# A two-block kernel: the first 64 modulation panels, summed on VectorE and TensorE, moved wholly to TensorE in 32-row column tiles

## What is computed

```
c_act = silu(c)                                    # (1, 2048)
mod = c_act @ w_ada + b_ada                        # w_ada: 2048 x 12288
sh1, sc1, g1, sh2, sc2, g2 = split(mod, 6)         # six vectors of 2048
h = rms_norm(x, norm_mix_g) * (1 + sc1) + sh1
proj = h @ w_in                                    # the first large product
...
x = x + g1 * (merged @ w_out)                      # first block, then the second
```

## Time and profile before

| | |
|---|---|
| median of three runs | 3482.86 us |
| the profiled execution | 3486.62 us |
| its span (first to last instruction) | 3484.8 us |
| VectorE busy | 2892.9 us, 83% |
| TensorE busy | 2341.4 us, 67% |
| GpSimd busy | 1267.6 us, 36% |
| ScalarE busy | 1008.8 us, 29% |

### The profile page before, as it was taken

The page is one execution under the profiler, slowest core; times in us unless marked ns, Lnnn a source line. Parts: engine busy times, 40 slices in busy tenths (PEclk is TensorE's granted clock), DMA queues, the critical chain, the costliest instruction groups (busy, mean ns, idle before and its releaser), DMA issues.

```text
span 3484.8 us, 37714 instructions
## 1 busy us (share of the span) xinstructions
PE 2341.4 (67%) x14550; PEld 1985.7 (57%) x14550; DVE 2892.9 (83%) x3487; ACT 1008.8 (29%) x1529; POOL 1267.6 (36%) x975
## 2 busy tenths in 40 slices
PE   8869999988999999998989889000044420003444
PEld 8858999977888888887979779000011110001111
DVE  7698867877897887888668767899999999998777
ACT  1404443434645454554565444000000000000000
POOL 6351101100110110110000001578867788886663
PEclk7779999999999999998999999555577765556766
DMA  9517978967887997984553346899999999999997
GB/s 363 205 32 269 348 255 305 339 254 247 301 327 266 329 320 273 323 311 164 175 169 110 105 149 223 343 398 420 420 420 420 420 420 421 421 420 421 420 420 319
DMA packets 223692, 1069.00 MB, mean 307 GB/s; under 512 B 24345, under 2 KB 30489, under 8 KB 157593
## 3 DMA queue, kind: packets, MB, share of 16 engines
q0 software_dynamic: 119808, 704.70, 51.1%
q1 hardware_dynamic: 103704, 361.89, 28.9%
HBM read 1062.82 MB, written 3.67 MB: 306 GB/s over the span
## 4 chain that ended last, share of the span: by engine, by line
PE 51%; DVE 18%; POOL 14%; DMA 11%; issue 4%; ACT 2%; DVEq 0%; POOLq 0%; SPq 0%; ACTq 0%
PE ps L597 50%; POOL wide L1751 6%; DMA wide<-in_up,idx_t 5%; DVE acts L2648 4%; POOL wide_b L1751 4%; POOL raws L1751 3%; DMA raws<-in_up,idx_t 2%; DMA wide_b<-in_up,idx_t 2%; DMA a_raws<-in_ada 1%; DVE wide L2576 1%; POOL a_acc L1751 1%; DVE a_raws L2505 1%; DVE a_acc L1791 1%; ACT acts L1291 1%; DVE raws_r L1767 1%
## 5 line engine op out<-in xcount | busy, mean ns | idle before, releaser
L597 PE MATMUL ps<-opa_both,w_hi 128*128 128x256 f32 (+1 forms) x5024 | 1152.0, 318 | 58.3 <-DVE opa_both L1867 31.5
L1767 DVE TENSOR_TENSOR raws_r<-raws,w_hi 128x1024 fp32r<-128x1024 f32 x607 | 729.9, 1223 | 233.3 <-ACT w_hi L1230 229.2
L597 PEld LDWEIGHTS ps<-opa_both,w_hi 128*128 128x128 f32 x5024 | 831.8, 194 | 124.5 <-issue 59.0
L597 PE MATMUL ps<-opa_both,raws_r 128*128 128x256 f32 x3152 | 883.7, 285 | 0.0
L1230 ACT ACTIVATE w_hi<-raws 128x1024 fp32r<-128x1024 f32 x607 | 638.0, 1057 | 672.8 <-PE ps L597 429.9
L597 PEld LDWEIGHTS ps<-opa_both,raws_r 128*128 128x128 f32 x3152 | 608.6, 193 | 7.4
L1666 POOL DMA_DIRECT2D a_raws<-in_ada x320 | 169.2, 529 | 1166.3 <-DVE a_acc L1791 920.0
L597 PE MATMUL ps<-opb_both,w_hi 128*128 128x512 f32 (+1 forms) x1952 | 578.2, 362 | 5.1 <-DVE opb_both L2471 4.8
L597 PE MATMUL ps<-opb_both,raws_r 128*128 128x256 f32 x1616 | 442.6, 282 | 0.0
L1791 DVE SCALAR_TENSOR_TENSOR a_acc<-a_raws,csil,a_acc 128x1024 f32<-128x1024 f32 x317 | 401.1, 1297 | 20.9 <-DMA a_raws<-in_ada 20.8
L597 PEld LDWEIGHTS ps<-opb_both,w_hi 128*128 128x128 f32 x1952 | 342.9, 190 | 58.7 <-DVE opb_both L2471 5.7
(11 more groups left out here) (445 smaller groups left out, 3340.2 us busy)
## 6 DMA issues: line engine op xcount, KB each, us to landing
raws<-in_w SPq DMA_DIRECT2D x607, 512.0 KB, 4.6
a_raws<-in_ada POOLq DMA_DIRECT2D x320, 512.0 KB, 5.7
a_raws<-in_ada SPq DMA_DIRECT2D x28, 512.0 KB, 9.1
raws<-in_ada SPq DMA_DIRECT2D x24, 512.0 KB, 10.8
acts<-in_ada SPq DMA_DIRECT2D x12, 512.0 KB, 8.8
x_res<-in_xT SPq DMA_DIRECT2D x1, 2048.0 KB, 13.0
out<-x_res SPq DMA_DIRECT2D x2, 1024.0 KB, 24.0
wide<-in_up,idx_t POOLq DMA_INDIRECT x109, 28.9
```

The lines of the kernel that those rows point to most:

```text
L597: return nc.tensor.matmul(out, lhs, rhs, start=start, stop=stop)
L1767: TT(w_lo[p % RAW].rearrange("p b n -> p (b n)"), raw[p % RAW], w_hi[p % HI][:, :, :].rearrange("p b n -> p (b n)").bitcast(F32), ALU.subt ...
```

## The change

All 64 panels of group 0 are summed by TensorE with the panel as the moving operand. `first_steps` does two matmuls a panel, each with 512 moving columns; the stationary operand is `csil_rows[:, k, :]`, column k of `csil` repeated 32 times (made once by a new VectorE copy, in room that later belongs to `opa_both`). Half a panel goes to column tile j = 2(h mod 2) + half, so that two successive panels of one pair fill the four column tiles of a bank: bank 4 for h = 0 and 1, bank 7 for h = 2 and 3. Over k the matmuls accumulate in PSUM. Then `ada_rows(0, 4)` and `ada_fold(0)` make columns of the rows, as for the other groups. VectorE's 43 steps, `pair_sums` and the first matmul into bank 7 (with zeros from `stat`) are gone. Every place of group 0 is now released by TensorE alone, by one count per panel. The order of loads is the same.

Two tensors are made longer (`quarter` from 4 to 32 columns, `fold_r` from 128 to 256 bytes a partition), by which `raws`, `a_raws`, `a_acc`, `wide`, `acts` and `wide_b`, into which panels and gathered rows land, start at a multiple of 256 bytes; before, all of them started 32 bytes past one.

```
-ON_PE = [q for q in range(64) if q < 4 or q % 7 in (1, 4)]
+FIRST_STEPS = 64
...
 def place_free(q):
     before = [r for r in range(q) if PLACES[r] == PLACES[q]]
-    return STEPS[before[-1]][:2] if before else None
+    return before[-1] + 1 if before else None
...
-fold_r = sb("fold_r", [P, 2, 4, 4])
+fold_r = sb("fold_r", [P, 2, 32])[:, :, 0:16].rearrange("p r (c s) -> p r c s", c=4)
...
+csil_rows = wide[:, 5, 1024:1536].rearrange("p (k m) -> p k m", k=DC)
...
+            def first_steps(q0, q1):
+                for q in range(q0, q1):
+                    h, k = first_group(q)
+                    pe.wait_ge(aland[PLACES[q]], 16 * USE[q])
+                    for half in range(2):
+                        j = 2 * (h % 2) + half
+                        m = mm(ps[32 * j:32 * j + 32, (4, 7)[h // 2], :], csil_rows[:, k, :],
+                               place[PLACES[q]][:, half * 512:(half + 1) * 512], k == 0, k == DC - 1)
+                    m.then_inc(S["adan"], 1)
...
-            mm(ps[:, 7, 0:32], ident, stat[:, 0, :], True, False)
-            pe.wait_ge(S["csl"], 2)
-            direct_steps(0, 8)
+            pe.wait_ge(S["csl"], 3)
+            first_steps(0, 8)
             norm(0)
-            direct_steps(8, 44)
-            pair_sums(0, STEPS[31][1] if 31 not in ON_PE else STEPS[30][1])
-            direct_steps(44, 64)
-            pair_sums(2, BY_DVE).then_inc(S["adaps"], 1)
+            first_steps(8, 64)
+            ada_fold(0)
...
+            V.tensor_copy(csil_rows, csil[:, 0, :].unsqueeze(2).broadcast_to([P, DC, 32])).then_inc(S["csl"], 1)
...
-            ada_steps(0, 16)
-            norm_rows(lambda j: ada_steps(16 + 4 * j, 20 + 4 * j))
-            ada_steps(48, 64)
+            norm_rows()
             rest_to(2)
+            ada_rows(0, 4)
             ada_cols(0)
```

More of the change, by code:

```diff
@@ L285 @@
 CON_N = (("ident", P), ("swap", P), ("rope_cos", T), ("rope_sin", T), ("causal", 3 * P), ("cmp_add", 2 * 16),
-         ("cmp_mul", 2 * 16), ("bucket", 384), ("iota16", 16), ("fold", 32), ("quarter", 4))
+         ("cmp_mul", 2 * 16), ("bucket", 384), ("iota16", 16), ("fold", 32), ("quarter", 32))
 def _consts():
@@ L355, in constants @@
     put("fold", np.tile(np.eye(32, dtype=np.float32), (4, 1)))
-    put("quarter", np.repeat(np.eye(4, dtype=np.float32), 32, 0))
+    put("quarter", np.tile(np.repeat(np.eye(4, dtype=np.float32), 32, 0), (1, 8)))
     put("iota16", np.broadcast_to(np.arange(16, dtype=np.float32), (P, 16)))
@@ L537, in load_a @@
                 if place_free(q):
-                    name, count = place_free(q)
-                    sp.wait_ge(S[name], count)
+                    sp.wait_ge(S["adan"], place_free(q))
                 half, k = first_group(q)
@@ L543, in load_first @@
             def load_first(p):
-                name, count = STEPS[[q for q in range(64) if PLACES[q] == HALVES + p][-1]][:2]
-                sp.wait_ge(S[name], count)
+                sp.wait_ge(S["adan"], [q for q in range(64) if PLACES[q] == HALVES + p][-1] + 1)
                 load_w(p)
@@ L680, in ada_sums @@
             def ada_sums(g, banks):
-                pe.wait_ge(S["ada"], 64 * (g + 1) - len(ON_PE))
+                pe.wait_ge(S["ada"], 64 * (g + 1) - FIRST_STEPS)
                 pe.wait_ge(S["adacol"], g)
@@ L691, in ada_fold @@
             def ada_fold(g):
-                pe.wait_ge(S["adafold"], g)
+                pe.wait_ge(S["adafold"], g + 1)
                 for i in range(4):
@@ L1664, in load_a @@
                 if q >= EARLY + HALVES:
-                    pool.wait_ge(S["ada"], q - HALVES + 1 - len(ON_PE))
+                    pool.wait_ge(S["ada"], q - HALVES + 1 - FIRST_STEPS)
                 pool.dma_start(a_raw[q % HALVES], a["ada"][q]).then_inc(bland[q % HALVES], 16)
@@ L1774, in ada_steps @@
                 for q in range(q0, q1):
-                    if q in ON_PE:
-                        continue
                     g, k, h = q // 64, q % 64 // HALVES, q % HALVES
[L1778 to L1782, removed]
-                    else:
[L1784 to L1791, removed]
+                    dve.wait_ge(bland[h], 16 * ((q - EARLY) // HALVES + 1))
+                    c = csil[:, g // 3, k:k + 1]
+                    if k == 0:
+                        ins = TS(a_acc[:, h, :], a_raw[h], c, None, ALU.mult)
+                    else:
+                        dve.wait_ge(S["ada"], q - HALVES + 1 - FIRST_STEPS)
+                        ins = STT(a_acc[:, h, :], a_raw[h], c, a_acc[:, h, :], ALU.mult, ALU.add)
                     ins.then_inc(S["ada"], 1)
             def ada_rows(g, b0):
-                dve.wait_ge(S["adarow"], g)
+                if g:
+                    dve.wait_ge(S["adarow"], g)
+                else:
+                    dve.wait_ge(S["adan"], FIRST_STEPS)
                 wide_e = a_acc[:, 0, :].rearrange("p (r a i) -> p r a i", r=2, i=32)
@@ L1802, in ada_rows @@
                     ins = TT(fold_e[:, r], fold_r[:, r].unsqueeze(1).broadcast_to([P, 4, 4, 4]),
-                             cst("quarter").unsqueeze(2).unsqueeze(2).broadcast_to([P, 4, 4, 4]), ALU.mult)
+                             cst("quarter")[:, 0:4].unsqueeze(2).unsqueeze(2).broadcast_to([P, 4, 4, 4]), ALU.mult)
                     if r == 0:
@@ L1823, in ada_cols, with norm_rows @@
                    ALU.add).then_inc(S["adacol"], 1)
-            def norm_rows(beside):
+            def norm_rows():
                 dve.wait_ge(S["ss"], 1)
@@ L1831, in norm_rows @@
                 for j in range(8):
-                    beside(j)
                     s = slice(2 * j, 2 * j + 2)
```

## The result

The changed kernel ran in 3448.94 us (median of four, 3446.68 to 3451.09), 35.0 us under the kernel before, whose median is 3483.97 with one more run added. The ratio is 0.9897, 95% interval [0.9879, 0.9916]. The forecast was 3467 us, range 3456 to 3477: the direction was right, and of the 35.0 us gained it had 15.8. The profiled execution's span fell from 3484.8 to 3445.6 us, by 39.2.

What follows compares the result with a forecast made beforehand. The first stage was taken as bound by loads waiting for their places, not by DMA's rate. Loads 10.8 us and tail 5.0 us made 15.8 us, taking the median from 3482.86 to 3467.1 us, range 3456 to 3477.

Steps and rivals of the forecast that it cites:

- the one on alignment: Landing places of panels and gathers: starting them at a multiple of 256 bytes was taken to gain 0.
- fitted 6.9 ns: Fixed part of a piece's DMA time, from panels of 4 KB pieces at 411 GB/s and gathers of 8 KB at 420.
- The bound of 24 us: Gathers: alignment can take no more than a piece's fixed part, 2.2% of their 1100 us.
- The rows of 1 KB pieces: Loads to `sg` (aligned) landed in 5.1 us, to `acts` (32 bytes past) in 5.7; nearest rows on alignment, mostly latency.
- The rival on alignment: Gathers: one unused beat a piece saved, 4.2 us more, 3463 us; by the whole bound 3443; chance 0.12.
- Loads and places: Group 0 loads: places released in time, 411 GB/s from 24 us on, last panel at about 100.6, 10.8 us earlier.
- The tail: From last panel's landing to the end of `gain`: 6.1 us instead of 11.14, 5.0 less (6.2 at the high clock).
- That all the rest shifts whole: From the first block's product on, everything waits for `gain` and shifts by the full 15.8 us.
- The slower rival: Group 0 sums on TensorE: column tiles don't overlap, low clock stays, 1.9 us a panel, 23 us slower, 3506; chance 0.06.

Runs made afterwards that it cites:

- a1: The changed kernel with the two lengthened tensors at their old lengths, landing places again 32 bytes past a multiple of 256, sums still on TensorE: 3469.21 us, ratio 0.9958.
- b2: The kernel before with the first `pair_sums` moved behind the step of panel 57 instead of panel 43: 3483.25 us, ratio 0.9997.

## Why the prediction was wrong

*The step that failed* is the one on alignment: "I take 0, since the rows of both sizes fit one fixed cost, which is what a piece would have anyway". Both rates came from pieces at the same 32 bytes past a multiple, so the fit could not tell what the place costs. What the runs showed in its place: 17.2 us less in the gathers by the trace, 20.3 in all when done alone. Nor does the place's cost come out of the fitted 6.9 ns: with the rates on the multiple, 420 and 427, the same fit still has 2 x 156.0 - 307.0 = 5.1 ns, since a piece of 4 KB lost 3.5 ns (159.5 to 156.0) and one of 8 KB 5.1 (the rates are rounded to 1 GB/s, so these are good to some tenths of a ns). The bound of 24 us held, though not by its reason; giving it a chance of 0.12, and only a third of its size in the range, was the mistake. The rows of 1 KB pieces, by the prediction's own words mostly latency, could not speak for or against it.

*The rival on alignment* had the sign, the stage and the condition (a share of 1.01). Its price of 4.2 us was a quarter of the measured one.

*Loads and places.* Right in mechanism: gaps gone, the rate the bound. In size, a1 is the clean test: the last panel at 102.48 instead of 100.6, so 9.0 us won of the 10.8 summed. The sum took the bytes ahead of the last landing as the same, and they were not. What still came behind it, in the kernel before and in a1:

```profile
111.40:118.00 6.60, 2.87 (x14) 2.87 (x14) 6.53 (x4) 0.00 (x0) 6.44 (x4) 0.50 0.37 149
```

```profile
102.48:106.00 3.52, 1.05 (x4) 0.14 (x4) 2.33 (x2) 0.00 (x0) 0.00 (x0) 0.96 0.19 77
```

That is 0.98 MB before and 0.27 MB in a1: with the queue full, 0.7 MB more of the first weights came ahead of the last panel, 1.7 us at 410 GB/s.

*The tail.* 5.0 us in a1 and in the changed kernel, against 6.1 at the low clock, with which the forecast went, and 4.9 at the high: the term was mis-sized by the clock. The forecast took 0.50 from the old stretch; the row of 24 to 96 us has 1.00 now, and a lone panel's step took 1.08 us where 1.0 was worked out for that clock. So the tail won 11.14 - 5.0 = 6.1 us instead of 5.0. With 9.0 from the loads that makes 15.1 against 15.8: that a1's time agrees so well with the forecast is in part luck, two errors of opposite sign.

*That all the rest shifts whole* held for a1 (15.1 us at `gain`, 15.2 in the time, within the spread of the runs) but is not a rule of this kernel, as b2 shows.

*The slower rival*, column tiles that don't overlap at a low clock, did not occur. Nor did its condition last: among the panels the granted clock was low only from about 16 to 23.3 us, ahead of `norm(0)`. Four panels, sixteen instructions, came in that part, and took 5.48 us, 1.37 a panel and not 1.9 (a line of the timeline and one of the stretches):

```profile
17.96 5.48 PE L578 MATMUL ps<-raws,wide 128*32 128x512 f32 x16 [4.59 <-DMA raws<-in_ada]
```

```profile
20.00:23.30 3.30, 3.30 (x12) 0.38 (x8) 1.86 (x9) 3.28 (x4) 0.00 (x0) 0.53 1.03 417
```

From 23.3 us to the last panel it was 1.00. The timeline after `norm(0)`, where panels were waiting, has two panels in 1.07 us, the time that one takes alone; of the next four, in 3.03 us, the last had only just landed, at 34.16:

```profile
30.48 1.07 PE L578 MATMUL ps<-raws,wide 128*32 128x512 f32 x8
...
32.22 3.03 PE L578 MATMUL ps<-a_raws,wide 128*32 128x512 f32 x16
...
37.86 1.05 PE L578 MATMUL ps<-raws,wide 128*32 128x512 f32 x4 [1.32 <-DMA raws<-in_ada]
```

A wait between two panels did not keep their tiles apart.

## What to carry to other kernels

Where a stage has DMA's share at 1.0, GB/s is a number to explain, not a ceiling: two rates read at one and the same start of the landing place cannot tell what the place costs, and a bound that can't be excluded belongs in the range whole. A queue's waits are worth looking at only where the stretch's rate falls. And moving one tensor moves all that are allocated behind it: before a difference is put down to the edit, the starts of the landing places and of TensorE's operands should be held fixed or varied by themselves.

## What the runs showed of the hardware that was not expected

- Landings of 8 KB pieces ran at 427 GB/s at a multiple of 256 bytes, at 422 for 64 and 128 bytes past one, at 420 for 32; 4 KB pieces (the panels) at 420 against 410 for 32.
- TensorE's matmuls of 256 columns in the large products came every 119.4 ns with weights and streamed operand at the same distance from a multiple of 256, every 117.0 ns with one of the two kinds of weights 32 bytes off the operand, and every 115.9 ns with both: 3449 us became 3424 without any instruction changed.
- An instruction of VectorE that takes 1.23 us otherwise took 2.29 us in b2 while GpSimd worked beside it.
